# Prices in a list scheduler: a change of ACT table priced at twice as much, and the DVE scalar-tensor-tensor formula split by operand place and width

## What is computed

```python
u = rms_norm(h, g_pre)
proj = u @ w_in                      # c_b c_c c_x c_z | q k v r lr_f lr_b | m_a m_b
y_conv = c_b * conv3(c_c * c_x) * silu(c_z)
p_conv = y_conv @ w_out_c
g_f = log_sigmoid(lr_f @ w_gate_f + b_f) / 16      # and g_b, per direction
o = gla(q, k, v, g_f) + reversed gla(q, k, v, g_b) # 4 heads, chunked, running state
y_gla = rms_norm(o, gla_g) * silu(r)
p_gla = y_gla @ w_out_g
merged = sigmoid(m_a) * p_conv + sigmoid(m_b) * p_gla
out = h + rms_norm(merged @ w_out, g_post)
```

## Time and profile before

| | us |
|---|---|
| median of 3 runs | 2888.99 |
| the runs | 2888.59, 2888.99, 3308.2 |
| the profiled execution | 2888.13 |
| its span on the slowest core, first to last instruction | 2886.6 |
| PE busy | 2828.3 (98%) |
| DVE busy | 1966.9 (68%) |
| ACT busy | 1355.8 (47%) |
| POOL busy | 735.7 (25%) |

### The profile page before, as it was taken

How to read it: one execution, slowest core, us unless ns; L and a number is a source line. 1 busy time by engine, 2 the same in 40 slices (tenths; PEclk the granted TensorE clock), 3 DMA queues, 4 the chain that set the end, 5 groups by cost and what they waited for, 6 DMA issues and landing times.

```text
span 2886.6 us, 53876 instructions; the slowest of 8 cores (2879.5 to 2886.6 us)
## 1 busy us (share of the span) xinstructions
PE 2828.3 (98%) x15980; PEld 1455.7 (50%) x15980; DVE 1966.9 (68%) x3095; ACT 1355.8 (47%) x2589; POOL 735.7 (25%) x1147
## 2 busy tenths in 40 slices
PE   6999999999999999999999999999999999999998
PEld 4555544444455555444446555444445655544443
DVE  5676673566777778666677778765667787866566
ACT  6775651232466664223256675323335666522222
POOL 4323223131222222222232222112223231211212
PEclk9999999999999999999999999999999999999999
DMA  8767548884642323566473322357456323245434
GB/s 199 136 118 119 116 78 207 244 222 123 203 113 75 76 74 83 158 189 193 135 219 78 79 70 75 104 174 222 142 156 181 83 69 76 72 136 155 132 121 153
DMA packets 351708, 386.54 MB, mean 134 GB/s; under 512 B 209328, under 2 KB 223152, under 8 KB 351424
## 3 DMA queue, kind: packets, MB, share of 16 engines
q1 hardware_dynamic: 337888, 357.72, 43.9%
q0 software_dynamic: 13536, 25.37, 6.0%
HBM read 298.70 MB, written 65.60 MB: 126 GB/s over the span
## 4 chain that ended last, share of the span: by engine, by line
PE 90%; DVE 3%; issue 2%; DMA 2%; ACT 1%; SPq 1%; POOL 0%; DVEq 0%; POOLq 0%; ACTq 0%
PE ps L479 90%; DMA sb_GR<-x 1%; DMA sb_SM<-sb_GR 1%; DVE sb_GR L505 0%; ACT sb_AT L496 0%; DMA sb_W<-w_all 0%; DVE sb_TF L509 0%; SPq L540 0%; DVE sb_CS L509 0%; DMA sb_onT<-x 0%; DVE sb_onT L509 0%; DVE sb_CS L505 0%; DVE sb_AT L505 0%; SPq L536 0%; DVE sb_TB L509 0%
## 5 line engine op out<-in xcount | busy, mean ns | idle before, releaser
L479 PE MATMUL ps<-sb_uT,sb_W 128*128 128x512 bf16 (+2 forms) x7840 | 1637.3, 366 | 2.3 <-DVE sb_AT L523 1.4
L479 PEld LDWEIGHTS ps<-sb_uT,sb_W 128*128 128x128 bf16 (+1 forms) x7840 | 709.2, 98 | 809.2 <-issue 30.0
L496 ACT ACTIVATE sb_CS<-ps 128x512 f32<-128x512 f32 (+2 forms) x512 | 272.9, 538 | 639.5 <-PE ps L479 578.6
L505 DVE TENSOR_TENSOR sb_CS<-ps,sb_CS 128x512 f32<-128x512 f32 (+1 forms) x464 | 315.2, 689 | 244.0 <-PE ps L479 165.5
L479 PE MATMUL ps<-sb_GR 128*128 128x512 bf16 (+2 forms) x1792 | 348.8, 318 | 1.8 <-DVE sb_GR L505 1.5
L509 DVE SCALAR_TENSOR_TENSOR sb_CS<-sb_CS,sb_convw 128x512 f32<-128x512 bf16 x256 | 208.9, 820 | 104.3 <-ACT sb_CS L496 93.2
L479 PE MATMUL ps<-sb_onT,sb_W 128*128 128x512 bf16 x1024 | 240.7, 379 | 2.0 <-DMA sb_W<-w_all 1.8
L479 PE MATMUL ps<-sb_V,sb_uT 128*128 128x256 bf16 x2048 | 235.9, 273 | 0.0
L505 POOL TENSOR_TENSOR sb_GR<-sb_CS 128x512 bf16<-128x512 f32 x64 | 88.4, 1381 | 575.1 <-DVE sb_CS L509 359.0
L479 PEld LDWEIGHTS ps<-sb_GR 128*128 128x128 bf16 x1792 | 163.6, 98 | 139.4 <-issue 4.4
L514 POOL TENSOR_SCALAR sb_stat<-sb_stat 128x2 f32<-128x2 f32 (+2 forms) x257 | 70.1, 273 | 585.3 <-ACT sb_TB L496 272.2
(11 more groups left out here) (137 smaller groups left out, 3175.4 us busy)
## 6 DMA issues: line engine op xcount, KB each, us to landing
sb_W<-wsc SPq DMA_DIRECT2D x412, 256.0 KB, 2.8
sb_W<-wst SPq DMA_DIRECT2D x168, 256.0 KB, 2.8
sb_onT<-x SPq DMA_DIRECT2D x56, 512.0 KB, 6.0
sb_GR<-x SPq DMA_DIRECT2D x44, 512.0 KB, 5.6
sb_W<-w_all POOLq DMA_DIRECT2D x80, 256.0 KB, 5.7
wsc<-sb_W SPq DMA_DIRECT2D x80, 256.0 KB, 5.4
y<-sb_GR SPq DMA_DIRECT2D x36, 512.0 KB, 3.6
sb_ycT<-x SPq DMA_DIRECT2D x28, 512.0 KB, 5.2
```

The costliest lines, as they stand in the source:

```text
L479: S.add("pe", lambda e: e.matmul(out, lhsT=lhsT, rhs=rhs, start=start, stop=stop, skip_group_check=more), r, w, cost=max(0.025, free_n(rhs ...
L496: S.add("act", lambda e: e.activation(out=out, in_=in_, func=func, **kw), r, w, table=TABLE.get(func), cost=0.17 + 0.82e-3 * free_n(in_) + ...
L505: S.add(eng, lambda e: e.tensor_tensor(out=out, in0=a, in1=b, op=op), r, w, cost=ecost(eng, free_n(out), narrow(out, a, b)))
```

## The change

Two numbers and a formula change. A change of ACT table is priced at 2.6 us instead of 1.3. A DVE scalar-tensor-tensor instruction was priced 0.21 us + 1.05 ns per element; now it is 0.15 if it reads PSUM, else 0.25, + 1.05 ns per element, + 0.08 at exactly 512 elements.

```diff
         if table is not None and table != self.table:
-            cost += 1.3
+            cost += 2.6
             self.table = table
...
-                  cost=0.21 + 1.05e-3 * free_n(out))
+                  cost=(0.15 if any(k[0] == "ps" for k in r) else 0.25) + 1.05e-3 * free_n(out) + 0.08 * (free_n(out) == 512))
```

## The result

The changed kernel is slower: 6.9% by the comparison made with the prediction (ratio 1.0691, 95% interval 1.0644 to 1.0738), and 6.4% when it was run once more beside the experiments (1.0638, 1.0619 to 1.0657). Its profiled execution took 3083.52 us against 2888.13 before. The forecast was 3010 us, range 2955 to 3065: the sign was right, the time lies outside the range. In some executions all cores of a die show a lower clock and take longer, whatever the kernel; the times and ratios here are those of the others.

What follows compares the result with a forecast made beforehand. PE was taken to bound the kernel, busy 2828.3 of 2886.6 us. Demand 70 + 25.5, DVE idle time 39, less 15 of vanishing waits, plus clock 8, gave 127.5 on 2888.13: 3016, taken as 3010 us, range 2955 to 3065.

Steps and rivals of the forecast that it cites:

- five stretches: Places where PE's waits end with DVE: one near the end of phase 1 in entries 1 to 3, two in entry 0.
- the demand term: DVE's work less PE's matmuls: 49.5 - 26.1 = 23.4 us per stretch in entries 1 to 3 (70 us), 25.5 in entry 0.
- DVE's idle time: DVE standing idle inside the five stretches, three terms, together 39 us added to the time.
- the scans' waits on ACT: Fourth scans wait for ACT behind the third half's last scan: 3.3 us, 13 in the four stretches that have it.
- the score blocks: PE, ACT and DVE taking turns at each score block: 2.5 us a stretch, 13 us in all.
- DVE's own last update: An update following another waits 0.17 to 0.18 us for it: 15 pairs in each of five stretches, 13 us.
- where the stretch begins: In entries 1 to 3, from head 2's second-half forward states to the bank that its last backward update frees.
- DVE over 85% busy: Sign of being right: in the stretches DVE is over 85% busy, with PE near 50%.
- 25 to 35 us: PE's waits ending with DVE, on `sb_SB` or masked scores, in each of the three like stretches of entries 1 to 3.
- If they end with a DMA or POOL, I have the wrong engine.: Sign of being wrong: PE's waits in the stretches end with a DMA or POOL instead of DVE.
- The clock, +8 us: Slower matmuls behind stalls: 1.7 us a stall, two for each of five stretches, less five present ones.
- PE itself slow: Rival: PE held at 1.2 GHz in the stretches, 4 x 18 = 72 us more, 3080 us; chance 0.06.

## Why the prediction was right in sign and wrong in size

- **Right: the place and the cause.** Table loads 37 as forecast, five stretches, PE waits of 173 us (140 or more), everything else at 0.215 us a projection. The table price alone gives the loss. The 45 us of table loads saved brought nothing that shows. The rule of the Trainium skill (ScalarE: Activation LUTs, section Table sets: the hidden batching unit), to do all activations of one table set before the next, is what this order comes nearer to, and the run with the table price alone, 39 loads instead of 72, is 6.2% slower.
- **Right: the demand term.** 49.5 us of DVE work forecast, 49.97 measured in the same part, and there 13 us less of that work gave 8 to 10 us back.
- **Wrong: DVE's idle time, "together 39 us; the bounds are nothing and twice that".** This is the step that failed, and of it the size. In the part summed DVE idles for 17.0 us in entry 1, against 7.8 forecast and an upper bound of 15.6 a stretch. The terms that I named were about right: 3.8 us for the scans' waits on ACT (3.3 forecast), 3.5 at the score blocks (2.5), 2.3 for DVE's own last update (2.6). What I had put at nothing is 3.1 us at the gate multiplications, waiting for ACT's exponentials, 1.9 for PE, 1.4 for POOL and 1 in pieces too short for the list.
- **Wrong as well: where the stretch begins.** I began it at head 2's second half. The first 23 us, with no filler either, lose 7.9 us more: PE's first wait of 5.19 us, and matmuls at a granted clock of 0.85. Of the miss (3069 to 3075 us against the sum of 3016), three times 7.9 us come from here and three times 8 to 9 from the idle time in the part summed.
- **Wrong: "DVE over 85% busy", and "25 to 35 us" of PE waits that end with DVE.** DVE is 72% busy (64.7 of 90.2; 75% in the part summed), with ACT at 55%. PE's waits in the stretch come to 37.5 us on core 0, and only 14.5 of them end with DVE; 12.9 end with the DMA and 10.1 with ACT.
- **"If they end with a DMA or POOL, I have the wrong engine."** The largest group does end with a DMA, `sb_KT`, 46.4 us, and the sign was partly true. The transposition (3.2 us from issue to landing in the median) is the last hop behind exponential, scan and multiplication. But the first of these waits in a stretch stayed when scans and multiplications were cut (5.64 us against 5.19), because the transposition stands behind a weight load in the DMA queue. The longest stayed as well (7.01 against 6.98). The stretch shortened by 9.3 us at other waits, more than half of it at the masked scores (4.41 against 7.36) and the fourth gates (1.50 against 3.67).
- **The clock, +8 us: too small, but by some 12 us and not by 60.** The rival "PE itself slow" had 72 us for it and 3080 us in all, nearest to the profiled time, and PE's busy time on the slowest core did rise by 71.5. That agreement is luck: on undisturbed cores it rose by 55 to 62 us, and lifting half of the fall brought about 10. The rival had the right number for the wrong reason, and only the run told them apart.
- **The rounding.** The sum was 3016 and I took 3010 because "one wait can cover another". The measured time is above the sum; the rounding went the wrong way.

## What to carry to other kernels

Where several engines work in turn with nothing beside them, sum the path through their hand-overs, one dependent instruction after the other, and not only the busiest engine's work: here that engine was busy for 72% of the stretch. (That such a sum gives the length was not tried.) Where such a path ends in a DMA, look at what stands ahead of it in its queue. When PE's busy time grows under the same matmuls, do not add it to the new waits as a cost of its own; slow matmuls between waits mostly used up wait here. And a list scheduler's price is no knob with a direction: 1.0, 1.3 and 2.6 us gave 80, 72 and 39 table changes and times of 0.997, 1 and 1.062, and the price nearest the traced 1.283 us was within 0.3% of the best.

## What the runs showed of the hardware that was not expected

- Two cores of eight had a granted clock of 0.81 with PE full, behind a stretch of waits: 127 matmuls in 30 us against 139 on core 0. A pair of cores was longer in all four executions of that comparison and in none of the four of the later one. What brought it on was not tried.
- A lower clock in a stretch of waits costs little: a mean of 0.78 to 0.80 against 0.90 was worth 1.2 us of 89.
- A DMA transposition whose data was ready by 1058.79 was issued at 1061.45, behind a weight load in the same queue, and the wait of 5.64 us on it did not get shorter with faster gates.
- A DVE memset of 128x2048 bf16 takes 1765 ns, the subtraction of two such tiles 1216.
